# First merged block of the expert lane loaded ahead of the opening's last stores, its residual a unit later, high query heads first in the second tile

## The reference

```python
merged = gates[:, :, 0] * o_fox + gates[:, :, 1] * o_conv + gates[:, :, 2] * o_mem
x = x + merged @ w['w_out']
x = x + peer(rmsnorm(x, w['norm2']), ...)

# peer, for a block of 128 tokens xb, 8 heads, 128 + 128 keys, 16 experts a head
q = (xb @ w_q).reshape(B, PEER_HEADS, 2, PEER_DK // 2)
s1, s2 = q[:, :, 0] . keys1, q[:, :, 1] . keys2
v1, i1 = lax.top_k(s1, 16); v2, i2 = lax.top_k(s2, 16)
top, pos = lax.top_k(v1 + v2 of all 256 pairs, 16)
g = softmax(top)
act = gelu(xb . u[idx], exact)
out = sum over h, k of (g * act) * v[idx]
```

## Time and profile before

| | us |
|---|---|
| median of 3 runs | 3797.9 |
| lowest, highest | 3795.76, 3809.41 |
| the profiled execution's own time | 3813.22 |
| its span in the profile | 3811.4 |
| PE busy | 3379.8 (89%) |
| DVE busy | 3013.4 (79%) |
| POOL busy | 2215.7 (58%) |
| ACT busy | 1346.0 (35%) |
| DMA | 1224.40 MB, mean 321 GB/s |

### The profile page before, as it was taken

The page is one execution under the profiler, slowest core; times in us unless marked ns, Lnnn a source line. Parts: engine busy times, 40 slices in busy tenths (PEclk is TensorE's granted clock), DMA queues, the critical chain, the costliest instruction groups (busy, mean ns, idle before and its releaser), DMA issues.

```text
span 3811.4 us, 45212 instructions
## 1 busy us (share of the span) xinstructions
PE 3379.8 (89%) x14054; PEld 2302.9 (60%) x14054; DVE 3013.4 (79%) x5990; ACT 1346.0 (35%) x2728; POOL 2215.7 (58%) x1831
## 2 busy tenths in 40 slices
PE   8999899899999859997999999999797896978855
PEld 7787555443434446665788787888574482754822
DVE  4598663477878858999988897979577799898965
ACT  5235674122532213333444444444322121222210
POOL 6221243155556546777766665666566586675876
PEclk9999999899999979998999999999898998989989
DMA  6415665699899979999999999999999899898899
GB/s 206 123 55 136 150 182 199 232 336 339 336 395 363 332 292 365 378 384 376 409 410 395 393 409 384 399 401 404 363 377 369 300 325 364 292 370 300 281 369 355
DMA packets 443309, 1224.40 MB, mean 321 GB/s; under 512 B 65250, under 2 KB 153478, under 8 KB 442047
## 3 DMA queue, kind: packets, MB, share of 16 engines
q0 software_dynamic: 239616, 872.52, 60.6%
q1 hardware_dynamic: 177162, 313.45, 23.7%
q10 hardware_dynamic: 26293, 35.54, 2.7%
HBM read 1129.03 MB, written 92.31 MB: 320 GB/s over the span
## 4 chain that ended last, share of the span: by engine, by line
PE 46%; DVE 14%; issue 8%; POOL 7%; DMA 6%; ACT 1%; SPq 1%; ACTq 0%; DVEq 0%; another core or an unknown queue 0%; POOLq 0%
PE open_q_and_scores_ps L2807 18%; PE open_sums_ps L1915 7%; DVE late_x L3272 4%; PE open_q_and_scores_ps L2856 4%; PE open_h_T_ps L1929 4%; POOL late_v_rows L2665 3%; POOL late_u_rows L2665 3%; PE open_h_T_ps L2785 3%; PE open_sums_ps L2888 3%; DVE late_u_rows L3249 2%; PE open_h_T_ps L2791 2%; DMA late_v_rows<-in_peer_v,table_twin_idx 1%; DMA late_u_rows<-in_peer_v,late_kept_idx 1%; PE open_sums_ps L1855 1%; DMA open_weight_columns<-in_w_in 1%
## 5 line engine op out<-in xcount | busy, mean ns | idle before, releaser
L2665 POOL DMA_INDIRECT late_v_rows<-in_peer_v,late_kept_idx x573 | 613.6, 1071 | 219.4 <-issue 166.4
L2652 POOL DMA_INDIRECT late_u_rows<-in_peer_u,late_kept_idx x320 | 476.3, 1488 | 267.2 <-DVE late_dots L3249 184.0
L3249 DVE CUSTOM_DVE_ANT_0 late_u_rows<-late_u_rows,open_rows_ps 128x1024 f32<-128x1024 f32 x432 | 522.0, 1210 | 9.8 <-DMA late_u_rows<-in_peer_u,late_expert_idx 9.2
L3272 DVE SCALAR_TENSOR_TENSOR late_x<-late_v_rows,late_weights,late_x 128x1024 f32<-128x1024 f32 x368 | 471.3, 1281 | 9.1 <-DMA late_v_rows<-in_peer_v,late_expert_idx 7.2
L2807 PE MATMUL open_q_and_scores_ps<-table_h_T_upper,table_u_T_upper 128*128 128x512 f32 x1024 | 426.3, 416 | 0.0
L2807 PE MATMUL open_q_and_scores_ps<-table_h_T_lower,table_u_T_upper 128*128 128x512 f32 x1024 | 407.6, 398 | 0.0
L2807 PE MATMUL open_q_and_scores_ps<-table_h_T_upper,table_u_T_lower 128*128 128x512 f32 x1024 | 404.8, 395 | 0.0
L2665 POOL DMA_INDIRECT late_u_rows<-in_peer_v,late_kept_idx x259 | 312.5, 1207 | 139.3 <-issue 73.6
L1828 POOL DMA_INDIRECT open_u_rows<-in_peer_u,late_expert_idx x115 | 163.5, 1422 | 256.6 <-DVE late_dots L2268 129.1
L2888 PE MATMUL open_sums_ps<-late_v_rows,late_diag 128*128 128x512 f32 (+1 forms) x460 | 241.1, 666 | 76.1 <-DMA late_v_rows<-in_peer_v,late_kept_idx 33.6
L2888 PE MATMUL open_sums_ps<-late_u_rows,late_diag 128*128 128x512 f32 x364 | 188.3, 661 | 109.1 <-DMA late_u_rows<-in_peer_v,late_kept_idx 62.6
(11 more groups left out here) (462 smaller groups left out, 7838.0 us busy)
## 6 DMA issues: line engine op xcount, KB each, us to landing
table_u_block<-in_peer_u SPq DMA_DIRECT2D x128, 512.0 KB
scr_scores<-table_scores SPq DMA_DIRECT2D x32, 1024.0 KB
open_weight_columns<-in_w_in SPq DMA_DIRECT2D x64, 256.0 KB
table_first_scores<-scr_scores SPq DMA_DIRECT2D x4, 4096.0 KB
table_second_scores<-scr_scores SPq DMA_DIRECT2D x4, 4096.0 KB
front_w_raw<-in_w_in SPq DMA_DIRECT2D x48, 256.0 KB, 5.6
scr_m<-open_gated SPq DMA_DIRECT2D x42, 256.0 KB
late_v_rows<-in_peer_v,late_kept_idx POOLq DMA_INDIRECT x573
```

The source lines that it names most:

```text
L2652: pool.indirect_dma_start(u[k % U_RING][:], None, io["peer_u"][0], bass.IndirectOffsetOnAxis(ap=rows_of(n), axis=0)).then_inc(s_u[k % U_RI ...
L2665: pool.indirect_dma_start(slot[:], None, io["peer_v"][0], bass.IndirectOffsetOnAxis(ap=rows_of(m), axis=0)).then_inc(arrived, 16)
L3249: dve.tensor_tensor_reduce(u[k % U_RING][:], u[k % U_RING][:], h2_rows, 1.0, 0.0, ALU.mult, ALU.add, dots[:, n % COLS:n % COLS + 1]).then_ ...
L3272: dve.scalar_tensor_tensor(rows[:], slot[:], weight_of(m), rows[:], ALU.mult, ALU.add).then_inc(s_vsum, 1)
```

## The change

Three things are moved; no arithmetic is added or taken away.

1. The merged rows of block 1 of `m` (tile 1) are loaded by SP inside the opening, ahead of the last stores of the last unit, as soon as PE's last product is done, and into `h2_next` instead of `h2`. `turn_merged(1)` reads them there.
2. On DVE and ACT the residual, square and norm of tile 1 come one unit later (heads 2 and 3 instead of 1 and 2 on DVE; ACT's square in head 3).
3. In the second tile (R = 8 to 15) the heads run in the order 4 to 7, 0 to 3, so that the half of the query weights that is in SBUF already is used first. The scores are stored under their true head.

```diff
+HEAD_AT = [R - R % NH + (R + NH // 2) % NH if R // NH == 1 else R for R in range(HEADS)]
+HALF_FIRST = (FIRST_KEPT, NH + NH // 2)
...
+        def load_first_merged(sp):
+            last = next(u for u in reversed(range(UNITS_OPEN)) if unit(u)[1] == 2)
+            sp.wait_ge(s_uprod, S0 + 2 * UNITS_OPEN)
+            for g in (2 * last, 2 * last + 1):
+                sp.wait_ge(s_mst[g % GATED_RING], S0 + 16 * (g // GATED_RING + 1))
+            sp.dma_start(L.h2_next[:], scr["m"][1]).then_inc(L.s_m, 16)
...
+            if u + 1 == UNITS_OPEN:
+                load_first_merged(sp)
             for h in range(2):
...
         def load_merged(t):
-            if t >= 2:
-                sp.wait_ge(s_hturn, S0 + t)
-                sp.wait_ge(s_h2out.sem, s_h2out.start + 16 * min(t - 1, SHORT))
-            else:
-                sp.wait_ge(s_hturn, S0 + 1)
-                sp.wait_ge(s_place, S0 + 1)
+            sp.wait_ge(s_hturn, S0 + t)
+            sp.wait_ge(s_h2out.sem, s_h2out.start + 16 * min(t - 1, SHORT))
...
             if t > 1:
                 sp.wait_ge(s_place, S0 + t)
+            else:
+                sp.wait_ge(s_mturn, S0 + 2)
             sp.dma_start(h2_next[:], scr["h2"][t]).then_inc(s_h2in.sem, 16)
...
-        load_merged(1)
         load_x_new(1)
...
-                src = h2[:, k * P:(k + 1) * P] if t else done.gated[...]
+                src = (h2_next if t == 1 else h2)[:, k * P:(k + 1) * P] if t else done.gated[...]
...
-                if R in (4, 8):
-                    L.w_q[R % NH // 4].wait(pe)
-                columns = L.w_q[R % NH // 4].buf[:, :, R % 4 * 2 * NK:(R % 4 + 1) * 2 * NK]
+                H = HEAD_AT[R]
+                if R in HALF_FIRST:
+                    L.w_q[H % NH // 4].wait(pe)
+                columns = L.w_q[H % NH // 4].buf[:, :, H % 4 * 2 * NK:(H % 4 + 1) * 2 * NK]
...
-            act.dma_start(scr["side"][R], L.side_stage[i % 2][:])
+            act.dma_start(scr["side"][HEAD_AT[R]], L.side_stage[i % 2][:])
...
-                    if t < NE and h == (2 if t == 0 else 6):
+                    if t < NE and h == (3 if t == 0 else 6):
                         square(t + 1)
...
+            if t == 1:
+                dve.wait_ge(s_hturn, S0 + 1)
             dve.wait_ge(s_inv, S0 + t + 1)
...
-                    if t < NE and h == (1 if t == 0 else 5):
+                    if t < NE and h == (2 if t == 0 else 5):
                         residual(t + 1)
-                    elif t < NE and h == (2 if t == 0 else 6):
+                    elif t < NE and h == (3 if t == 0 else 6):
                         normed(t + 1)
```

10 lines of the change are left out of this document (5 added, 5 removed).

## The result

The changed kernel takes 3772.3 us in the median of 6 executions (3769.21 to 3787.21), the kernel before beside it 3797.72 (6 executions, 3793.84 to 3809.41): a ratio of 0.9935 [0.9914, 0.9957], 25.4 us less. Two repeats beside new executions of the kernel before gave 0.9929 [0.9911, 0.9946] and 0.9938 [0.9920, 0.9956]. The profiled executions have spans of 3811.4 and 3785.4 us, 26.0 apart. The forecast of 3772.0 is met within 0.3 us, and one of its terms is nevertheless wrong by its whole size.

The account below looks back on a forecast made before the run. The prediction took the chain through a DMA hole at 1344 to 1369 us, up to DVE's second residual, as the bound. Its terms, -13.0 - 1.3 - 7.4 - 5.8 + 1.5, gave -26.0 us: median 3772, range 3764 to 3787.

Parts of the forecast that it names:

- Term 1: End of the opening: first merged block loaded ahead of the last stores, turned at 1330.7 instead of 1343.65, saving 13.0 us.
- Rival C: Opening: the early load shares the queue's end with the last stores, lands near 1343; only -7 to -13 us; chance 0.08.
- Term 2: PE right behind query 4: without the pause, transposes and next query run at the upper clock, saving 1.3 us.
- Term 3: DVE: residual and norm one unit later, two steps fill idle time ahead of the residual; low half issued 7.4 us earlier.
- The norm behind it: First block's norm at 1361.4 to 1362.9: DVE idles 4 us for ACT's square and root, without setting the end.
- Term 4: Second tile: four high heads first, two queries move into the wait for the second merged block; worth zero.
- term 6: PE behind the second merged block: restart at a lower clock after a wait of about 15 us, costing 1.5 us.
- Term 5: SP's queue, low half and stores: POOL's pause leaves it some 4.6 us alone, saving 5.8 us (bounds 0 and 8.9).
- rival A: SP's queue gets no relief from POOL's pause: -20.2 us, 3777.7, second block's turning near 1395; chance 0.17.
- The busy share of DVE from 1420 to 1790: DVE behind the second residual: no new idle time expected; a share below 0.97 would show the forecast wrong.
- Rival B: From 1344 us the DMA engines' transfers bind: -19.4 or -15.5 us (3782), down to -13; chance 0.14.
- Rival D: Low half starves beside POOL's gathers: the 5.2 MB take over 50 us; at 85 GB/s +11 us, 3809; chance 0.03.

## Why the number was right and one step wrong

*Term 1, the early load (13.0 us).* Right. From the mark to the first turning: 35.6, 35.8 and 35.6 us before, 22.3, 22.4 and 22.1 after, **13.4 us**. The block was there before PE was done with query 4. Rival C falls.

*Term 2, no pause of PE (1.3).* Right. From the mark to the first projection the gain is 14.8 to 16.3 us in the three pairs, 1.4 to 2.9 beyond term 1; with the transposes at 1.04 and the query at 3.62 us, at a granted clock of 1.00 (2.4 GHz) where the transposes before had 0.50 (1.2 GHz), it is 1.4 in the first pair.

*Term 3, the late residual (7.4).* Right in size: low issued 55.9 us behind the mark without it and 48.7 with it. Low issued itself came 23.3 us sooner, from 72.0 to 48.7 in the means, where I had 21.7. The wait before the first residual came out at 4.32 us plus 0.96 for a row and 0.61 unattributed, 5.9 together. I had named 7 to 9 as the sign, which did not fit my own terms: 27.06 - 13.0 - 1.3 - 7.4 is 5.4.

*The norm behind it.* The 4 us of waiting for the root are 5.76. ACT was late by one thing I had not seen: it held the copy for query 7 until the side scores' store had landed, and that 5.50 us transfer, on full DMA engines, is in the chain. The low half stands ahead of the norm and did not suffer. The store of h2 was issued 7.3 us behind the low half (1361.34 to 1368.66) instead of 4.7 (1379.04 to 1383.77), which costs nothing as long as the 4 MB are moving ahead of it: with the true head order the store went out 6.4 us behind the low half, and the block was issued 5.0 us behind the low half's landing, as in the kernel before.

*Term 4, the high heads first (0).* Right, 3773.66 against 3772.75. The reason is right too, since the same wait moves from one place to another. By the marks it costs 3 us at the second residual (116.7 against 113.7), part of which is term 6. I had not priced what it makes possible.

*Term 5, relief on SP's queue (5.8).* **Wrong; this is the step that failed**: "some 4.6 us alone on the queue", and with it the price 8.9 x 4.6 / 7.1. (By its own two times, 1359 and 1364.1, the pause was 5.1 us.) From low issued to block issued it took 31.6, 30.5 and 31.9 us, against 30.2, 30.4 and 30.7 before: 0.9 us longer in the mean, not 5.8 shorter. POOL did pause, for 5.91 us here and 7.20 and 7.59 in the repeats:

```profile
1363.78 0.94 POOL L2673 DMA_INDIRECT late_v_rows<-in_peer_v,late_expert_idx  x1 [0.31 <-issue]
1370.63 1.74 POOL L2660 DMA_INDIRECT late_u_rows<-in_peer_u,late_expert_idx  x1 [5.91 <-DVE late_dots L3260]
```

But SP's queue was not alone. In exactly these 5.91 us the DMA engines ran at a share of 1.03 and 403 GB/s, and the queue of the gathers, q0, had almost as much of it as SP's, q1, although POOL issued nothing. Only in the two microseconds from 1373.34, 8.6 us behind the start of the pause, did SP's queue have 87.5% of the engines. The busy times of the pause, the two queues in it, and the two queues in 1373.34 to 1375.34:

```profile
1364.72:1370.63 5.91, 1.94 (x8) 1.57 (x8) 3.45 (x6) 2.50 (x5) 0.00 (x1) 0.77 1.03 403
...
q1 hardware_dynamic: 309, 1.14, 49.1%
q0 software_dynamic: 285, 1.06, 44.6%
...
q1 hardware_dynamic: 189, 0.70, 87.5%
q0 software_dynamic: 47, 0.13, 16.2%
```

POOL had issued a gather each 1.2 to 2 us since 1340, and what it had issued was still being moved. In the row that I took the 7.1 us from the earlier trace rows, the weights were issued 5.8 us into the pause, and in the last 1.75 us ahead of them the engines moved 9 GB/s, so the backlog was gone:

```profile
1306.50:1308.25 1.75, 1.75 (x6) 0.55 (x4) 1.72 (x8) 0.00 (x0) 0.00 (x0) 1.00 0.02 9
```

I mistook the end of issuing for the end of moving. What SP's queue had moved, counted from low issued (MB, q1 in `--dma` of these windows):

| | after 4 us | after 16 us | after 24 us | after 28 us | block issued, us |
|---|---|---|---|---|---|
| before | 0.07, 0.05, 0.11 | 2.55, 2.53, 2.56 | 4.19, 4.15, 4.18 | 5.01, 4.98, 5.03 | 30.2, 30.4, 30.7 |
| changed | 0.22, 0.09, 0.09 | 2.84, 3.11, 2.89 | 4.37, 4.66, 4.47 | 5.10, 5.18, 5.14 | 31.6, 30.5, 31.9 |

So there was a relief, late and smaller: 0.29 to 0.56 MB at 16 us, which at the 0.21 MB per us of the kernel before are 1.4 to 2.7 us. It was lost again by the landing. From 22 to 26 us the side-score transfers of ACT, which queries 8 and 9 now put there, have 13.2 to 14.0% of the engines, and SP's queue has 43 to 47% where it had 52 before; at 28 us some 0.6 us are left, and the end of the last store comes later still. How the last part is lost is open. With the true head order, where POOL paused for 3.79 us, no such moment shows at all: from 10 us behind low issued on, SP's queue stays at 50 to 52% until 28 us. POOL held back altogether gives 16.4 us, so the mechanism exists, and this pause is too short for it.

The Trainium skill, "DMA: Bandwidth & Descriptors", section "Queues, rings and completion order", lets each engine take turns between queues with work. The prediction set 173 GB/s of 409 against the even share, and that was a misreading: 173 is the mean over all 30.2 us, and in the first 4 of them SP's queue had 4 to 7% and the gathers issued before it 93 to 97%. From 4 to 28 us it had 51.2 to 51.6% and the gathers 50.8 to 51.2%, in all three profiles of the kernel before: the even share. By that rule the term would have been 2 to 3 us, about what the relief was at 16 us; the rule does not say that the relief comes 8 us behind the pause, nor that it is lost by the end.

*Term 6, the cold restart (+1.5).* Right: from the second turning to the second residual 27.3 us before, and 29.9, 28.8 and 29.7 after, +1.5 to +2.6, in the mean 2.2. In the 18.43 us of standing the granted clock had fallen to 0.50 (1.2 GHz). The transposes took 1.97 us at that level and the query 5.14, in the mean at 0.70; the projection behind them ran at 1.00 (2.4 GHz).

*The sum.* Terms 1 to 4 and 6 make -20.2, and the marks show 20.4 to the second residual: 23.3 to low issued (21.7 forecast), -0.9 on the queue (5.8 forecast), 0.2 to the turning, and -2.2 behind it (-1.5 forecast). This is **rival A**, which I gave 0.17. Its turning was to be near 1395 and is at 1400.18 in an execution whose mark is 4.6 later: 1395.6. The sign that I named for the turning spoke for A. In median time the three comparisons give 25.4, 26.8 and 21.9 us, a mean of 24.7. The 4 us beyond 20.4 I did not find. They are not in the stretch that was changed; from the second residual to the end the three profiles of before have 2367.5, 2370.4 and 2356.0 us and those of the changed kernel 2355.4, 2349.8 and 2354.3. No profile of the kernel before is on record from the chip on which the two repeats of the changed kernel ran. So whether they are real or scatter of chips stays **open**, and the agreement of 3772.3 with 3772.0 is partly luck: a false 5.8 stood for these 4 us and more.

*The busy share of DVE from 1420 to 1790* is the sign that I had set at 0.97 or more:

```profile
1420.00:1790.00 370.00, 325.72 (x1408) 248.40 (x1406) 355.45 (x760) 129.82 (x274) 266.16 (x217) 0.94 0.97 361
```

It is 0.96, so by my own sign the mechanism would be wrong. The sign was badly set: the kernel before has 0.96 in this window too (355.58 of 370 us), and the repeats of the changed kernel have 0.99 and 0.98. Behind the second residual at 1430.03 DVE is busy 0.98 of the time here, and 0.99 in the kernel before. The segment to the table stage has two levels, near 369 and near 372.5 us, in both kernels. They differ by one wait of DVE for the root that ACT makes: it is 3.5 us in the third profile of the kernel before and 3.6 here, both on the upper level, and at most 0.8 us in the profiles near 369. So nothing new starves there.

*Rival B, the transfers bind.* Half right: the engines were full from 1344 to 1420. But with full engines DVE still waited 15.35 us for the exps. ACT makes them, and ACT had itself stood for 17.58 us until PE turned the second merged block. With the block ahead of the low half the second residual comes 12.9 us sooner with the same bytes to move. What bound was which bytes went first. The Trainium skill, "DMA: Bandwidth & Descriptors", section "Specifications", gives about 358 GB/s for a core, as half of the 716 of a memory stack that two cores share; this program runs on one core, and the trace holds 406 over these 76 us.

*Rival D* falls: the 5.2 MB were through in 32 us, not 50.

## What to carry to other kernels

A pause of the engine that issues gathers is not a pause of the DMA engines: read the DMA share of the same window, queue by queue, before you credit a neighbour on another queue with the room. When a change fills a hole with transfers and they run full, look next at the order on the queue, and put the 512 KB that the chain waits for ahead of 4 MB that have slack. Here that gave another 11.9 us on one chip, and only together with a head order that alone gave nothing. And count from a mark ahead of the change in several profiles: a total can agree to 0.3 us with errors in it that cancel.

## What the runs showed that I had not expected

- A load on SP's queue first waits for the gathers issued before it, some 4 us here, and then shares the engines evenly with them: the 5.2 MB took 30.2 to 31.9 us beside them and 16.4 without.
- A small store can hold up three engines: the 128 KB of side scores took 5.50 us under full DMA engines, and ACT, DVE and PE waited one behind the other.
- Chips differ by 19 us on the same kernel (3798 and 3817 us), nearly as much as this change. A part of it lies in the closing stage: 185 to 190 us against 195 in the kernel before, 179 to 181 against 192 to 196 in the changed ones. The same edit, the second block first, gained 33.8 us on one of the chips and 20 on the other.
